# The first modulation sums of a two-layer encoder move from VectorE to TensorE, behind four products that nobody reads

## The reference

```python
c_act = jax.nn.silu(c)
for l in range(DEPTH):
    mod = c_act @ w_ada[l] + b_ada[l]
    x = _layer(x, mod, ...)
# in _layer:
shift, scale, gate = jnp.split(mod, 3, axis=-1)
h = _rmsnorm(x, norm_w) * (1.0 + scale[:, None]) + shift[:, None]
proj = h @ w_in
```

## Time and profile before

| | us |
|---|---|
| median of 3 runs | 1145.28 |
| lowest, highest | 1143.53, 1145.81 |
| the profiled execution | 1143.7 |
| its span, first to last instruction | 1141.9 |
| TensorE busy | 1117.4 (98%) |
| VectorE, GpSimd, ScalarE busy | 660.1, 566.4, 529.8 |

### The profile page before, as it was taken

One profiled execution on the slowest core, in us unless ns is written; L12 is line 12 of the kernel. 1 busy time (PEld: TensorE's weight loads), 2 busy tenths in 40 slices (PEclk: granted clock), 3 DMA queues, 4 the chain that ended last, 5 costly groups with the idle time before them and its releaser, 6 DMA issues.

```text
span 1141.9 us, 15266 instructions
## 1 busy us (share of the span) xinstructions
PE 1117.4 (98%) x5843; PEld 920.5 (81%) x5843; DVE 660.1 (58%) x823; ACT 529.8 (46%) x928; POOL 566.4 (50%) x409
## 2 busy tenths in 40 slices
PE   6999999999999999999999999999999999999996
PEld 5778888888888888887898788888788887888885
DVE  4716456579887546336870635665988854131375
ACT  5544366655445533223463535656545453232234
POOL 5535444445535546555814363444445535454464
PEclk8999999999999999999999999999999999999998
DMA  9656432235442455653303463224433523443332
GB/s 320 205 140 198 120 86 82 81 104 138 120 127 75 131 176 176 205 164 100 106 20 99 144 202 93 75 75 121 119 114 90 138 65 88 119 126 99 105 93 92
DMA packets 203337, 140.80 MB, mean 123 GB/s; under 512 B 11984, under 2 KB 191232, under 8 KB 203264
## 3 DMA queue, kind: packets, MB, share of 16 engines
q1 hardware_dynamic: 202488, 138.91, 42.0%
q10 hardware_dynamic: 776, 0.91, 0.3%
HBM read 136.64 MB, written 2.63 MB: 122 GB/s over the span
## 4 chain that ended last, share of the span: by engine, by line
PE 90%; POOL 4%; DVE 2%; SPq 1%; DMA 1%; ACT 1%; issue 1%; DVEq 0%; ACTq 0%; POOLq 0%
PE main L676 73%; PE psC L676 6%; PE psA L676 5%; PE psB L676 4%; POOL w_lo L594 3%; SPq L393 1%; DMA big<-in_w_ada 1%; PE psB L909 1%; PE psB L889 1%; DVE h_lo L1521 1%; DMA zs<-in_w_ada 0%; ACT w_hi L1089 0%; SPq L421 0%; DVE psC L1474 0%; DVE tmp L1516 0%
## 5 line engine op out<-in xcount | busy, mean ns | idle before, releaser
L594 POOL TENSOR_TENSOR w_lo<-raw,w_hi 128x512 fp32r<-128x512 f32 x344 | 509.3, 1500 | 538.6 <-ACT w_hi L1089 538.5
L676 PE MATMUL main<-h_hi,w_hi 128*128 128x512 f32 x976 | 390.0, 401 | 3.8 <-ACT h_hi L1089 2.9
L676 PE MATMUL main<-h_hi,w_lo 128*128 128x512 f32 x976 | 379.8, 390 | 0.0
L676 PE MATMUL main<-h_lo,w_hi 128*128 128x512 f32 x976 | 379.3, 390 | 0.0
L1089 ACT ACTIVATE w_hi<-raw 128x512 fp32r<-128x512 f32 x344 | 199.9, 623 | 309.6 <-PE main L676 175.0
L676 PEld LDWEIGHTS main<-h_hi,w_hi 128*128 128x128 f32 x976 | 183.6, 188 | 51.9 <-issue 11.3
L676 PEld LDWEIGHTS main<-h_hi,w_lo 128*128 128x128 f32 x976 | 183.2, 188 | 39.1
L676 PEld LDWEIGHTS main<-h_lo,w_hi 128*128 128x128 f32 x976 | 183.3, 188 | 37.8 <-issue 1.9
L1682 DVE SCALAR_TENSOR_TENSOR misc<-main,cols,misc 128x511 f32<-128x511 f32 (+2 forms) x96 | 71.9, 749 | 60.9 <-ACT misc L1089 58.3
L676 PE MATMUL main<-y_hi,w_hi 128*128 128x512 f32 x256 | 100.5, 393 | 0.0
L676 PE MATMUL main<-y_lo,w_hi 128*128 128x512 f32 x256 | 99.7, 389 | 0.0
(11 more groups left out here) (277 smaller groups left out, 1414.6 us busy)
## 6 DMA issues: line engine op xcount, KB each, us to landing
raw<-in_w_in SPq DMA_DIRECT2D x124, 512.0 KB, 3.9
xbc<-in_w_ada SPq DMA_DIRECT2D x16, 512.0 KB, 4.8
zs<-in_w_ada SPq DMA_DIRECT2D x16, 512.0 KB, 4.3
raw<-in_w_pc SPq DMA_DIRECT2D x16, 512.0 KB, 3.8
raw<-in_w_out SPq DMA_DIRECT2D x16, 512.0 KB, 3.6
zs<-in_w_ada SPq DMA_DIRECT2D x16, 256.0 KB, 7.9
xbc<-in_w_in SPq DMA_DIRECT2D x8, 512.0 KB, 7.4
big<-in_w_ada SPq DMA_DIRECT2D x16, 256.0 KB, 7.3
```

The lines of the kernel that those rows point to most:

```text
L594: nc.gpsimd.tensor_tensor(lo_b[:, cut, :], raw_b[:, cut, :], hi_b[:, cut, :].bitcast(F32), ALU.subtract).then_inc(s_split[b], 2 * BT_ // kt)
L676: return nc.tensor.matmul(o, a, b_, start=start, stop=stop)
```

## The change

`BY_PE` becomes a number of blocks for each quarter: TensorE takes all eight blocks of quarter 0 and the last four of quarter 1 (`quarter_rows`, which replaces `first_rows`). `OWN` leaves three blocks of quarter 2 to ScalarE and GpSimd and none elsewhere. VectorE has none of quarter 0, four blocks of quarter 1, five of quarter 2 and the addition of the products, and all eight of quarter 3, of which four come behind `h_low`. Before the main products stand four products of 256 columns into `psB`, whose result is overwritten. The first pair of k-tiles gets an order of its own (`first_pair`). On ScalarE the first `h_high` moves ahead of some `w_hi`. The reloads of the slabs wait for other readers.

```diff
@@ -70,11 +70,9 @@
 QUARTERS = 4
 HALF = SEQ // 2
 FOLD = D // 32
-OWN = (0, 3, 4, 3)
-BY_PE = (2, 3)
-PROD0 = tuple(sum(OWN[:q]) for q in range(QUARTERS))
-PADD0 = tuple(sum(max(n - 1, 0) for n in OWN[:q]) for q in range(QUARTERS + 1))
-ADAQ = (KT - len(BY_PE),) + tuple(KT - n + 1 for n in OWN[1:])
+OWN = (0, 0, 3, 0)
+BY_PE = (KT, KT // 2, 0, 0)
+ADAQ = tuple(KT - m - n + (n > 0) for m, n in zip(BY_PE, OWN))
 ADAQ0 = tuple(sum(ADAQ[:q]) for q in range(QUARTERS + 1))
 ADA0 = ADAQ0[QUARTERS]
...
@@ -378,16 +376,12 @@
 
                 n = D // QUARTERS
                 for g in range(KT // 2):
-                    if q == 2 and 2 * g in BY_PE:
-                        sp.wait_ge(s_adap, 1)
-                    elif q == 2:
-                        sp.wait_ge(s_adau, (2, 0, 4, 6)[g])
-                    if q == 3:
-                        for k in (2 * g, 2 * g + 1):
-                            if k < OWN[1]:
-                                sp.wait_ge(s_prod, PROD0[1] + k + 1)
-                            else:
-                                sp.wait_ge(s_adau, ADAQ0[1] + k - OWN[1] + (2 if k == KT - 1 else 1))
+                    if q == 2:
+                        sp.wait_ge(s_adap, g + 1)
+                    if q == 3 and 2 * g < KT - BY_PE[1]:
+                        sp.wait_ge(s_adau, ADAQ0[1] + 2 * g + 2)
+                    elif q == 3:
+                        sp.wait_ge(s_adap, g + 3)
                     cols_ = w_ada_t[0, 2 * g:2 * g + 2, :, 0:2 * D].rearrange("k p (w n) -> p k w n", n=D)
                     for w in range(2):
...
@@ -769,17 +760,17 @@
                 pe.wait_ge(s_adau, ADAQ0[q + 1])
                 for j in range(QUARTERS):
                     last = mm(quarter_ps[q][:, j:j + 1], quarter_acc[q % 2][:, j * P:(j + 1) * P],
-                              ones[:, 0:1], q > 0, q > 0 or j == QUARTERS - 1)
-                last.then_inc(s_adam, 1)
-
-            def first_rows():
-
-                pe.wait_ge(s_cact, 1)
-                pe.wait_ge(s_ada[BY_PE[0] // 2], 32)
-                for k in BY_PE:
+                              ones[:, 0:1], q > 1 or j == 0, q > 1)
+                if q > 1:
+                    last.then_inc(s_adam, 1)
+
+            def quarter_rows(q, g):
+
+                pe.wait_ge(s_ada[q % 2 * 4 + g], 32)
+                for k in (2 * g, 2 * g + 1):
                     for j in range(QUARTERS):
-                        last = mm(quarter_ps[0][:, j:j + 1], quarter_slab[0][:, k, j * P:(j + 1) * P],
-                                  fcol[:, k:k + 1], (k, j) == (BY_PE[0], 0), False)
+                        last = mm(quarter_ps[q][:, j:j + 1], quarter_slab[q][:, k, j * P:(j + 1) * P],
+                                  fcol[:, k:k + 1], (q, k, j) == (0, 0, 0), (k, j) == (KT - 1, QUARTERS - 1))
                 last.then_inc(s_adap, 1)
 
             def half_sums(half):
...
                                   ident[0:SH, 2 * i + e:2 * i + e + 1].broadcast_to([SH, 64]), hpar[:, 2, :])
                 last.then_inc(s_ds, 1)
 
-            def wide_high(k):
-
-                for i, (u, b) in enumerate(WIDE):
+            def wide_high(k, tiles=range(len(WIDE))):
+
+                for i in tiles:
+                    u, b = WIDE[i]
                     pe.wait_ge(s_hi[b], part_count(0, u, k // BT_, b))
...
@@ -817,10 +809,29 @@
                     pe.wait_ge(s_h, k + 1)
                     mm(wide_ps[i], w_bufs(0, u, b)[1][:, k, :], h_lo[:, k, :], False, False)
 
+            def first_pair():
+
+                for k in range(2):
+                    wide_high(k, range(3))
+                for k in range(2):
+                    wide_high(k, (3,))
+                for k in range(2):
+                    wide_low_weights(k, range(2))
+                for k in range(2):
+                    wide_high(k, range(4, 6))
+                wide_low_rows(0)
+                quarter_sums(1)
+                for g in (2, 3):
+                    quarter_rows(1, g)
+                for k in range(2):
+                    wide_low_weights(k, range(2, 4))
+                wide_low_rows(1)
+                for k in range(2):
+                    wide_low_weights(k, range(4, 6))
+
             def wide_pair(q):
-
                 a, b = 2 * q, 2 * q + 1
-                tiles = range(len(WIDE) - 1 if q == 0 else len(WIDE))
+                tiles = range(len(WIDE))
                 wide_high(a)
                 wide_high(b)
                 wide_low_weights(a, tiles)
...
@@ -854,13 +861,19 @@
                 last = nc.tensor.transpose(main[0][:, l * P:l * P + V_ROWS], stage_v[0:V_ROWS, l, :],
                                            ident[0:V_ROWS, 0:V_ROWS])
             last.then_inc(s_rT, 1)
-            first_rows()
+            pe.wait_ge(s_cact, 1)
+            quarter_rows(0, 0)
+            quarter_rows(0, 1)
             spread(psC0, rms, 1)
-            quarter_sums(0)
+            quarter_rows(0, 2)
+            quarter_rows(0, 3)
             pe.wait_ge(s_cols, 1)
             pe.wait_ge(s_xc, 2)
             pe.wait_ge(s_xca, 2)
-            for q in range(QUARTERS - 1):
+            for _ in range(4):
+                mm(psB[:, 512:768], ident[:, :], stage_x[:, 0, 0:256])
+            first_pair()
+            for q in range(1, QUARTERS - 1):
                 wide_pair(q)
             for i in range(len(WIDE)):
                 wide_end(i, KT - 2)
...
                 act.wait_ge(s_h32, h_count(l, k, half))
                 f(h_hi[:, k, tok], h_tmp[k % 4][:, tok], ACT.Identity, bias=mod[:, l, k:k + 1]).then_inc(s_hhi, 1)
 
-            def products(q):
-
-                for k in range(OWN[q]):
+            def products(q, ks):
+
+                for k in ks:
                     act.wait_ge(s_ada[q % 2 * 4 + k // 2], (q // 2 + 1) * 32)
-                    if q > 1 and k == 0:
-                        act.wait_ge(s_adau, ADAQ0[q] - 1)
-                    if k == 3:
-                        act.wait_ge(s_padd, PADD0[q] + 1)
-                    f(scaled[2 - k % 2] if k else scaled[0], quarter_slab[q % 2][:, k], ACT.Copy, scale=fcol[:, k:k + 1]).then_inc(s_prod, 1)
+                    f(scaled[k], quarter_slab[q % 2][:, k], ACT.Copy, scale=fcol[:, k:k + 1]).then_inc(s_prod, 1)
 
             act.wait_ge(s_cact, 1)
             x_out()
-            for u, b in WIDE[:4]:
-                w_hi_half(0, u, b, 0)
+            w_hi_half(0, 0, 0, 0)
+            w_hi_half(0, 0, 1, 0)
             h_high(0, 0)
+            w_hi_half(0, 1, 0, 0)
             h_high(0, 1)
+            w_hi_half(0, 1, 1, 0)
             w_hi_half(0, 2, 0, 0)
             w_hi_half(0, 2, 1, 0)
-            products(1)
-            products(2)
+            products(2, range(2))
             h_high(0, 2)
             h_high(0, 3)
+            products(2, range(2, 3))
             for u, b in WIDE:
                 w_hi_half(0, u, b, 1)
-            h_high(0, 4)
-            h_high(0, 5)
-            products(3)
-            h_high(0, 6)
-            h_high(0, 7)
+            for k in range(4, KT):
+                h_high(0, k)
             act.wait_ge(s_small, 16 * N_SMALL)
             f(hpar[:, 3, :], hpar[:, 1, :], ACT.Exp).then_inc(s_ea0, 1)
...
@@ -1460,9 +1468,10 @@
                 for n, k in ks:
                     dve.wait_ge(s_ada[q % 2 * 4 + k // 2], (q // 2 + 1) * 32)
                     part = quarter_slab[q % 2][:, k]
+                    end = k == KT - BY_PE[q] - 1
                     done = ADAQ0[q] + n
-                    if q > 0 and k == KT - 1:
-                        dve.wait_ge(s_padd, PADD0[q + 1])
+                    if end and OWN[q]:
+                        dve.wait_ge(s_padd, OWN[q] - 1)
                         dve.wait_ge(s_adau, done)
                         tt(psC1, psC1, scaled[0], ALU.add).then_inc(s_adau, 1)
                         done += 1
@@ -1471,7 +1480,7 @@
                     if n == 0:
                         ts_(psC1, part, fcol[:, k:k + 1], None, ALU.mult).then_inc(s_adau, 1)
                     else:
-                        stt(psC1 if k < KT - 1 else quarter_acc[q % 2], part, fcol[:, k:k + 1], psC1, ALU.mult, ALU.add
+                        stt(quarter_acc[q % 2] if end else psC1, part, fcol[:, k:k + 1], psC1, ALU.mult, ALU.add
                             ).then_inc(s_adau, 1)
 
...
@@ -1507,7 +1516,10 @@
                 modulation(l, unfolded[:, :], half * BT_, (half + 1) * BT_)
 
             def quarter_mod(q):
-                dve.wait_ge(s_adam, q + 1)
+                if q < 2:
+                    dve.wait_ge(s_adap, (4, 6)[q])
+                else:
+                    dve.wait_ge(s_adam, q - 1)
                 modulation(0, quarter_ps[q], 2 * q, 2 * q + 2)
 
...
@@ -1550,10 +1562,8 @@
             dve.wait_ge(s_cact, 1)
             x_copy(0)
             x_copy(1)
-            use_rows(0, ((0, 0), (1, 1)))
             mean_square(rms, s_xsq, PAIRS, sm[:, 4])
             root_of(rms, 1)
```

(9 more changed lines are left out.)

19 lines of the change are left out of this document (6 added, 13 removed).

## The result

The changed kernel takes **1155.61 us** in the median of six runs (1152.06 to 1157.35) against 1144.09 of the kernel before (1143.36 to 1145.81), a ratio of 1.0094 (interval 1.0076 to 1.0112). It is slower, by 11.5 us in the medians. Its profiled execution took 1153.36 us (span 1151.6), 9.7 more than the 1143.7 of the execution before. Each set has its own runs of the kernel before (medians 1144.09 to 1145.41), so runs of different sets are compared by their ratios.

The account below looks back on a forecast made before the run. TensorE, busy for 98% of the span, was taken to bound the kernel. Terms 6.0 - 1.6 + 3.4 - 1.5 + 1.1 = +7.4 us on the profiled 1143.7 gave 1151, with a range of 1145.0 to 1154.5.

Parts of the forecast that it names:

- start of the main products: After quarter 0's sums on TensorE and the unread products, first main product at 27.7 against 21.72 us: +6.0 us.
- main products at half clock after it: Clock rises near 28.9, so main products lose 0.6 us at half clock in place of 2.2: -1.6 us.
- half of quarter 1 by TensorE: 16 one-column products, 32 records, stand between main products with nothing to hide them: +3.4 us.
- standstills that go: TensorE's three gaps, for quarter 1's accumulator, h_hi of k = 2 and at 52.77, all vanish: -1.5 us.
- standstills that come: VectorE's eight rows of quarter 3 make TensorE wait 0.7, then 0.2 and 0.2 for k = 7: +1.1 us.
- behind the opening: What follows 61.4 us is TensorE-bound and moves with the opening; nothing added there.
- Does the clock fall?: In quarter 0, small products had not prevented the fall at 16.2 us, so the fall is taken as given.
- B: Rival: clock stays full through the opening, first main product at 22.6; +1.7 us, 1145.4; chance 0.20.
- C: Rival: clock falls already at 12.2 us, so all 64 records and the spread run at half; +11.2, 1154.9; chance 0.12.
- D: Rival: one-column products at half their price, main products start at 19.3; -3.3 us, 1140.4; chance 0.06.

Follow-up runs that it names:

- e8: The changed kernel unaltered, run again in a second set of four runs: 1153.34 us, ratio 1.0070.
- e6: e4 with quarter 1's 16 TensorE products also streaming 128 identity columns, their sums left out: 1150.42 us, ratio 1.0047.
- e7: Changed kernel with quarter 0 summed as in the kernel before; half of quarter 1 on TensorE and unread products kept: 1147.83 us, ratio 1.0034.
- e2: Changed kernel with all eight slab rows of quarter 1 back on VectorE, quarter 0 still on TensorE: 1152.61 us, ratio 1.0064.
- e3: Kernel before plus only the four unread 256-column products behind the sum of quarter 0: 1145.96 us, ratio 1.0008.
- e9: Kernel before with e10's edit, plus two unread products ahead of quarter 0's sum and four behind it: 1145.36 us, ratio 1.0002.
- e5: Changed kernel with eight main products placed between the sixteen one-column products of quarter 1, one ahead of every two: 1157.52 us, ratio 1.0107.
- e1: Changed kernel without its four unread products of 256 columns: 1156.8 us, ratio 1.009.
- e10: Kernel before with VectorE making h_lo of k = 0 and 1 before all its rows of quarter 1: 1143.72 us, ratio 0.9991.
- e4: Changed kernel with quarter 0's products from row 2 on streaming 128 identity columns, their sums left out: 1149.89 us, ratio 1.0041.

## Why the prediction was right or wrong

It forecast 1151, +7.4 against the profiled 1143.7, and gave slower 0.75. The direction and the first part of the mechanism (a half clock through quarter 0, records on TensorE's path) are as forecast; a second half clock, at quarter 1, was left out, and so the size is too small. The measured median, 1155.61, lies 1.1 us above the upper end of the range, 1154.5; the profiled execution (1153.36) and the median of all ten runs (1153.5) lie within. Of the 4.6 us between 1151 and that median, 2.4 stand in the profile and are explained by the terms; the other 2.2 are there because the profiled execution was shorter than the median.

| term | forecast | measured |
|---|---|---|
| start of the main products | +6.0 | +4.2 (25.95) |
| main products at half clock after it | -1.6 | -1.6 (rise at 27.2) |
| half of quarter 1 by TensorE | +3.4 | **+5.5** |
| half clock behind those records | not in the sum | **+1.4** |
| standstills that go | -1.5 | -1.5 |
| standstills that come | +1.1 | +0.7 |
| sum at the stage's end | +7.4 | +8.7 (by the ends: +8.5) |
| behind the opening | 0 | +1.2 |

**The step that failed** is *Half of quarter 1 by TensorE*. It priced the 32 records by eight that had run at full clock (0.91 and 0.80 us) and let the clock stay full behind the first rise. The clock fell within them: 1.5 us at 0.11 a record, 4.0 at 0.22. The 14 main products behind them took 42.67 - 38.05 = 4.6 us in place of 3.2. Together that is 6.9 against 3.4. In e8 the same step fails by less: the records took 3.57 us, as forecast, and the 14 products behind them 42.72 - 37.83 = 4.9 us, together 5.3 against 3.4. The second fall is in both profiles; whether it meets the records or the products behind them differs between executions. The evidence lay in the prediction: *Does the clock fall?* argued that small products had not kept the clock up at 16.2, yet asked this only of quarter 0. The same argument held for four times as many records at quarter 1. That the fall goes with the one-column form of these products is shown by e6 (no fall with 128 columns, 3.58 us for as many records); that it can come without quarter 0 on TensorE is shown by e7's profile. These products aren't the only place for a fall, though: in e2, e3 and e9 the clock also fell near quarter 1's sum, with no more one-column records there than the sum's eight and a wait of 1.2 to 3.1 us ahead of them, while in e6 it stayed full behind such a wait (1.56 us). What separates these cases is open.

That the profile came as near as 2.4 us is in part luck: the start of the main products, 1.8 too dear, and the new standstills, 0.4 too dear, hid 2.2 of the 3.5 us that this step lacks.

**Start of the main products:** mechanism right, size 1.8 us too large. The groups began at 12.04, not 12.25, the fall came at 17.0, not 16.2, and the groups behind it took 6.24 us, not 7.0; all this together makes 1.5 us at 22.75. The unread products took 3.2 us, 0.40 a record at half clock, not 3.5. That columns set their price and not the weight load was the right choice. How far this term is off depends on the execution: in e8 the main products began at 28.08, +6.4. e8's stage is no longer for it, since its second fall was shorter; whether an early first fall always goes with a short second one, two profiles don't show.

**The half clock after the start, the old standstills:** as forecast. **New standstills:** two were named, before the sum of quarter 3 and before h_hi of k = 6. They measured 0.42 (57.17 to 57.59) and 0.28 (61.33 to 61.61, by the pace of the products ahead), with a TensorE that came late. Where it comes on time, the first is 1.56 us (e6) and 1.64 (e5): VectorE's eight rows of quarter 3 are the next limit behind the clock. The working had a slip there: (16.70 - 14.12) / 3 is 0.86 us a row, not 0.83, so eight rows take 6.9 us and the forecast gap would have been 1.0.

**The rivals.** *B* (clock full, +1.7, 0.20) didn't occur. e6 made its condition true and gave its other terms their test: the first main product at 22.48 (forecast 22.6), the stage's end at +3.1. B was 1.4 too cheap; 0.9 of that is quarter 3's standstill, 1.56 where I had 0.7. The Trainium skill, TensorE: Matmul & The Clock Gate, "Why this matters for your kernels", asks only for no idle gaps between bursts of matmuls, and would have had B, since TensorE never idles from 12 us on. This trace disagrees: two falls, at 17.0 and 34.1, in stretches where TensorE is busy for all of the time. *C* (an early fall, +11.2, 0.12) had its condition in part in e8 and e1, with falls at 14.7 and 14.2, not 12.2, and in e8 not its price: the stage ended at +8.6. e1 ended at +11.1, near C's +11.2, but by a long second fall that C doesn't have. *D* (half price for one-column products) is refuted: 0.11 us a record at full clock, and nothing less in any dense row of them. The range was said to go from B's middle to C's, which are 1145.4 and 1154.9; its ends are 0.4 below these, and the median lies above C's middle too.

**The spread.** I left the difference between executions to the range's upper end, 1.6 us, from the runs of before. The six runs of the changed kernel spread by 5.3 us, the six beside them of the kernel before by 2.5. The mean granted clocks go with it. The shortest (1152.06) had 0.991, the longest (1157.35) 0.987; 0.4% of 1155 is 4.6 us. That the change itself widens the spread isn't shown: e8's four runs spread by 1.8 us, e2's four by 0.7, and 23 of the kernel before by 3.3. In some profiled executions the clock falls between 525 and 540 us too (e1, e6, e9, e10), which costs about 1.7 us and lies far behind anything that the change touches. It comes behind a standstill of 2.1 us in which TensorE waits for VectorE between the layers, but the kernel before and after have this standstill as well and no fall. Which conditions decide it was not found.

**Behind the opening, +1.2:** ScalarE's wait for a transfer in layer 1 was 6.58 us, before 5.47. It was 5.4 to 5.6 in e1, e2, e7, e9 and e10, 5.9 in e3 and 6.6 to 6.9 in e4, e5, e6 and e8. e8 and after agree, but so do e4 and e6 with other openings, while e1 and e2, near after in all else, are low. TensorE's wait for `w_lo` behind it goes with it: 0.9 us in after and e8, 1.1 to 1.3 in e4, e5 and e6, 0.3 in e3, none in the others. I found no part of the change that goes with it; its cause is open.

## What to carry to other kernels

Before work is moved to TensorE, ask how many columns each weight load streams: a sum by one-column f32 products pays 0.11 us for each of two records, as much as with 128 columns (e4), did not get cheaper between wide products (e5), and was followed here by a half clock for the products behind it. Price such work at both clocks, at every place where it stands and with the products behind it, not only at the first. And where an opening has several engines that take turns, a gain on one (a full clock, an earlier first product) is worth only what the next wait for another engine leaves of it: look up that wait before the edit.

## What was not expected of the hardware

- The clock falls under unbroken work. TensorE was busy 18.00 of 18.00 us from 12 to 30 and the mean grant was 0.72; with the same weights and 128 columns it was busy for 16.83 and had 1.00 (e4).
- One f32 product of one column takes two records of 0.11 us at full clock and two of 0.21 to 0.22 at half; with 128 columns it costs the same at full clock. Of 256 columns a record takes 0.40 at half clock.
- Four one-column records between two products of 512 columns cost their full 4 x 0.11 us (e5).
- The place of a fall moves by some 2 us between executions of one kernel (17.0 and 14.7), and falls far from any change (525 to 540 us) come in some profiles and not in others.

What was not tried: to keep true sums while many columns flow, say with the condition vector spread over 128 columns, or to give ScalarE its share of quarter 3 back in e6. By e6's stage end I estimate that the first could save up to 69.98 - 64.58 = 5.4 us; the second up to 1.3 us more (1.56 - 0.25). That would still leave the stage's end 1.8 us behind the kernel before.
